# A two-block transformer kernel: the first input projection in another order, and four additions behind another weight piece

## The reference

```python
h = rmsnorm(x, norm_mix)
proj = h @ w_in                      # the first input projection
(m_z, m_xbc, m_dt, b_qkv, c_qkv, c_f, d_q, d_kv, gate_logits) = split(proj)
y_a = mamba2_branch(m_z, m_xbc, m_dt, ...)       # convolution of m_xbc, then a state space scan
y_b = moba_attention(b_q, b_k, b_v, ...)
y_c = forgetting_attention(c_q, c_k, c_v, c_f + forget_bias)
y_d = sliding_window_attention(d_q, d_k, d_v, ...)
x = x + sum(sigmoid(gate_logits) * (branches @ w_branch)) @ w_out
h = rmsnorm(x, norm_ffn)
x = x + (silu(h @ w_gate) * (h @ w_up)) @ w_down     # the first feed-forward
x = rmsnorm(x, norm_final)
```

## Time and profile before

| what | us |
|---|---|
| median of 3 runs (lowest, highest) | 928.53 (926.15, 930.83) |
| profiled execution | 926.62 |
| its span | 924.8 |
| PE busy | 907.0 |
| DVE busy | 685.7 |
| ACT busy | 509.9 |
| POOL busy | 103.9 |

### The profile page before, as it was taken

How to read it: one execution, slowest core, us unless ns; L and a number is a source line. 1 busy time by engine, 2 the same in 40 slices (tenths; PEclk the granted TensorE clock), 3 DMA queues, 4 the chain that set the end, 5 groups by cost and what they waited for, 6 DMA issues and landing times.

```text
span 924.8 us, 15609 instructions
## 1 busy us (share of the span) xinstructions
PE 907.0 (98%) x6262; PEld 771.2 (83%) x6262; DVE 685.7 (74%) x1116; ACT 509.9 (55%) x807; POOL 103.9 (11%) x114
## 2 busy tenths in 40 slices
PE   8999999999999999999999899999999999999998
PEld 8998887787778788888888689888988788888886
DVE  5876546566777768888788769678867578888886
ACT  5654446557854466555555574646436455565551
POOL 1000000131004100111000000003350003330000
PEclk9999999999999999999999999999999999999999
DMA  9769842244456535555544442231000445555631
GB/s 323 304 133 283 313 182 91 100 174 147 173 212 239 184 120 206 201 198 187 182 182 130 171 163 91 92 104 80 3 3 24 162 182 182 182 193 196 228 113 46
DMA packets 16871, 149.78 MB, mean 162 GB/s; under 512 B 1744, under 2 KB 6224, under 8 KB 8352
## 3 DMA queue, kind: packets, MB, share of 16 engines
q1 hardware_dynamic: 14688, 140.24, 41.0%
q0 software_dynamic: 1296, 5.24, 3.2%
q10 hardware_dynamic: 816, 3.31, 0.9%
HBM read 144.59 MB, written 4.19 MB: 161 GB/s over the span
## 4 chain that ended last, share of the span: by engine, by line
PE 87%; DVE 5%; ACT 3%; issue 2%; POOL 1%; DMA 1%; ACTq 0%; DVEq 0%; POOLq 0%
PE bank L774 41%; PE bank L816 17%; PE bank L818 9%; PE bank L731 4%; PE bank L1622 3%; PE bank L994 1%; POOL HN L3470 1%; DVE W_LOW L2484 1%; PE bank L1031 1%; PE bank L1068 1%; ACT W_HIGH L1856 1%; PE bank L899 1%; PE bank L1489 1%; DMA PRM<-params_dram 1%; PE bank L1383 0%
## 5 line engine op out<-in xcount | busy, mean ns | idle before, releaser
L2484 DVE TENSOR_TENSOR W_LOW<-weights,W_HIGH 128x2048 fp32r<-128x2048 f32 (+1 forms) x97 | 219.6, 2265 | 75.0 <-ACT W_HIGH L1856 74.1
L1856 ACT ACTIVATE W_HIGH<-weights 128x2048 fp32r<-128x2048 f32 (+1 forms) x97 | 181.5, 1872 | 105.8 <-PE bank L774 101.8
L816 PE MATMUL bank<-OVER_BOTH,W_HIGH 128*128 128x512 f32 x608 | 211.6, 392 | 0.2 <-DVE W_LOW L2484 0.2
L818 PE MATMUL bank<-OVER_BOTH,W_LOW 128*128 128x256 f32 x608 | 170.0, 280 | 0.0
L816 PEld LDWEIGHTS bank<-OVER_BOTH,W_HIGH 128*128 128x128 f32 x608 | 114.1, 188 | 25.9 <-DVE W_LOW L2484 0.5
L818 PEld LDWEIGHTS bank<-OVER_BOTH,W_LOW 128*128 128x128 f32 x608 | 114.2, 188 | 0.0
L1794 ACT ACTIVATE ARENA<-bank 128x256 f32<-128x256 f32 x88 | 33.6, 383 | 101.8 <-PE bank L818 101.0
L774 PE MATMUL bank<-GATE_HIGH,FIRST_BOTH 128*128 128x512 f32 x256 | 85.9, 400 | 1.0 <-DVE RING_LOW L2657 1.0
L774 PEld LDWEIGHTS bank<-GATE_HIGH,FIRST_BOTH 128*128 128x128 f32 x256 | 48.1, 188 | 11.6 <-DVE RING_LOW L2657 1.7
L774 PE MATMUL bank<-W_HIGH,HID_LOW 128*128 128x512 f32 x146 | 56.9, 390 | 0.0
L774 PE MATMUL bank<-W_LOW,HID_HIGH 128*128 128x512 f32 x146 | 56.9, 390 | 0.0
(11 more groups left out here) (580 smaller groups left out, 1932.5 us busy)
## 6 DMA issues: line engine op xcount, KB each, us to landing
weights<-weights_dram SPq DMA_DIRECT2D x62, 2048.0 KB, 8.1
weights<-weights_dram SPq DMA_DIRECT2D x3, 1024.0 KB, 9.0
bias_rows_dram<-ARENA POOLq DMA_DIRECT2D x1, 3072.0 KB, 39.5
BIAS<-params_dram ACTq DMA_DIRECT2D x1, 1997.0 KB, 14.6
weights<-weights_dram SPq DMA_DIRECT2D x1, 1664.0 KB, 6.6
weights<-weights_dram SPq DMA_DIRECT2D x1, 1584.0 KB, 6.8
weights<-weights_dram SPq DMA_DIRECT2D x3, 512.0 KB, 5.5
X<-x_dram ACTq DMA_DIRECT2D x2, 512.0 KB, 4.6
```

Of the source, the lines that this page charges most:

```text
L816: pe.matmul(o[:, :].rearrange("p (q n) -> p q n", q=2), high, both[:, :, k, :], start=(k == 0), stop=False, skip_group_check=True)
L818: ins = pe.matmul(o[:, 0:S], low, both[:, 0, k, :], start=False, stop=(k == KD - 1), skip_group_check=True)
L1856: act.activation(part_of(like_source(piece_parts(k)[0], k), k), part_of(piece_source(k), k), ACT.Copy)\
L2484: dve.tensor_tensor(low, part_of(src, k), high.bitcast(F32), ALU.subtract)\
```

## The change

The list of the first projection's chunks and jobs gets the order 0, 1, 2, 5, 9, 3, 4, 6, 7, 8, 10 (`IN1_ORDER`). Chunks 3 and 4 become wide like 6, 7 and 8. PE runs 5 and 9 by tokens where 3 and 4 stood, and then, behind `xs_T` and `cb`, the five wide chunks; the transposes of the rates come behind the first wide one, chunk 3. On ACT and DVE the takes, high and low parts follow that order. Apart from this, step 1 of `extras` of the first feed-forward stands one piece later. The pieces keep their count; by places in the new order 10 and 11 are chunk 3, 12 and 13 chunk 4.

```diff
--- before.py
+++ after.py
@@ -41,7 +41,8 @@
 LEVELS = 7
 
 
-CHUNKS = [("in1", i, w) for i, w in enumerate([KD * 384] + [KD * 512] * 10)]
+IN1_ORDER = (0, 1, 2, 5, 9, 3, 4, 6, 7, 8, 10)
+CHUNKS = [("in1", i, KD * (512 if i else 384)) for i in IN1_ORDER]
 CHUNKS += [("gate", i, KD * 512) for i in range(8)]
 CHUNKS += [("branch", i, 4 * D) for i in range(4)]
 CHUNKS += [("out1", i, KD * 512) for i in range(2)]
@@ -62,10 +63,10 @@
     return [(0, j, t) for t in range(2) for j in range(2)] + [(i, j, t) for i in range(1, chunks) for j in range(2) for t in range(2)]
 
 
-WIDE_IN = (6, 7, 8)
+WIDE_IN = (3, 4, 6, 7, 8)
 TILES = {"in1": [(i, j, t) for i in WIDE_IN for j in range(2) for t in range(2)], "ffn1": tiles_of(FF1_CHUNKS),
          "ffn2": tiles_of(FF2_CHUNKS)}
-JOBS = [("in1", i, j, *t) for i in range(11) for j in range(2) for t in (((0,), (1,)) if i in WIDE_IN else ((),))]
+JOBS = [("in1", i, j, *t) for i in IN1_ORDER for j in range(2) for t in (((0,), (1,)) if i in WIDE_IN else ((),))]
 JOBS += [("gate", i, j) for i in range(8) for j in range(2)]
 JOBS += [("branch", i, j) for i in range(4) for j in range(4)]
 JOBS += [("out1", i, j) for i in range(2) for j in range(2)]
@@ -934,9 +935,9 @@
             f_job_split("in1", 1, 0, *first)
             wait_fill_out(pe, ("table",))
             f_job_split("in1", 1, 1, *first)
-            for i in (2, 3):
-                f_jobs_split("in1", i, *first)
-            f_jobs_split("in1", 4, *first)
+            f_jobs_split("in1", 2, *first)
+            for i in (5, 9):
+                t_jobs_split("in1", i, *first)
             pe.wait_ge(sem("conv_done"), 8)
             for tt in range(TT):
                 o = open_fill(("xs_T", tt))
@@ -948,12 +949,12 @@
                 o = open_fill(("cb", g))
                 pe.matmul(o[:, 0:S], XBC[:, 4 + g, 0:P], XBC[:, 6 + g, :], start=True, stop=True)
                 close_fill(pe.matmul(o[:, S:384], XBC[:, 4 + g, P:S], XBC[:, 6 + g, P:S], start=True, stop=True))
-            for i in range(5, 11):
+            for i in (*WIDE_IN, 10):
                 if i in WIDE_IN:
                     wide_in(i)
                 else:
                     t_jobs_split("in1", i, *first)
-                if i == 5:
+                if i == WIDE_IN[0]:
 
                     pe.wait_ge(sem("rates_cumulated"), 1)
                     o = open_fill(("dt_T",))
@@ -1970,24 +1971,18 @@
             act.wait_ge(sem("params_halved"), 1)
             convs(0, 8)
             split_high(9)
-            take(("in1", 3, 0), flat(CQ1[:, 0:2, :]), 0.125)
+            take(("in1", 5, 0), CV1[:, 0, :])
             split_high(10)
             act.activation(EALOG[0:NH, :], prm("a_log")[0:NH, :], ACT.Exp).then_inc(sem("a_ready"), 1)
             softplus_parts(0, SPT)
-            take(("in1", 4, 0), flat(CK1[:, 0:2, :]))
+            take(("in1", 9, 0), BV1[:, 0, :])
+            split_high(11)
             for g in range(2):
                 take_fill(("cb", g), CB[:, g, :], 384)
-            split_high(11)
-            split_high(12)
-            take(("in1", 5, 0), CV1[:, 0, :])
-            split_high(13)
             for n, (i, j, t) in enumerate(TILES["in1"]):
-                cross_out("in1", n, (i, j, t), 1.0 if i == 8 else 0.125)
+                cross_out("in1", n, (i, j, t), 1.0 if i in (4, 8) else 0.125)
                 if t:
                     split_high(PIECE_AT["in1", i, j] + 2)
-            split_high(20)
-            take(("in1", 9, 0), BV1[:, 0, :])
-            split_high(21)
             gate_high(0)
             for tt in range(TT):
                 o = job_arrived(act, ("in1", 10, tt))
@@ -2610,7 +2605,7 @@
             convs(0, 8)
             minus_abs(SPX, SPT)
             split_low(9)
-            take(("in1", 3, 1), flat(CQ1[:, 2:4, :]), 0.125)
+            take(("in1", 5, 1), CV1[:, 1, :])
             split_low(10)
             softplus(0, SPX, SPT, SPX)
             dve.wait_ge(sem("consts_in"), 16)
@@ -2620,16 +2615,13 @@
             dve.tensor_tensor_scan(FCUM, ones[0:NH, :], SPX[:, S:2 * S], 0.0, ALU.mult, ALU.subtract)\
                 .then_inc(sem("rates_cumulated"), 1)
             split_low(11)
-            take(("in1", 4, 1), flat(CK1[:, 2:4, :]), 1.0)
+            take(("in1", 9, 1), BV1[:, 1, :])
             dve.wait_ge(sem("rates_cumulated"), 1)
             rows = SM8[0:NH, 768:1280]
             link(dve.tensor_scalar(DECAY_PARTS[:, :], ones[:, 0:1].to_broadcast([P, 512]), 0.0, None, ALU.mult))
             link(dve.tensor_copy(DECAY_PARTS[0:NH, :], rows))
             dve.tensor_tensor(DECAY_PARTS[32:32 + NH, :], rows, DECAY_PARTS[0:NH, :].bitcast(F32), ALU.subtract)\
                 .then_inc(sem("rows_ready"), 1)
-            split_low(12)
-            split_low(13)
-            take(("in1", 5, 1), CV1[:, 1, :], 1.0)
             o = fill_arrived(dve, ("dt_T",))
             dve.tensor_copy(DTT, o[:, 0:TT * NH])
             fill_out(dve.tensor_scalar(KEY_RATES, o[:, TT * NH:2 * TT * NH], -1.0, None, ALU.mult), ("dt_T",))
@@ -2642,12 +2634,10 @@
                 fill_out(dve.tensor_tensor(dst[1], src, bc(prm("d_skip", 0, NH).unsqueeze(2), [P, NH, HD]), ALU.mult),
                          ("xs_T", tt))
             for n, (i, j, t) in enumerate(TILES["in1"]):
-                add_cross("in1", n, (i, j, t), {6: DQ1, 7: BQ1, 8: BK1}[i][:, 2 * j + t, :], 1.0 if i == 8 else 0.125)
+                add_cross("in1", n, (i, j, t), {3: CQ1, 4: CK1, 6: DQ1, 7: BQ1, 8: BK1}[i][:, 2 * j + t, :],
+                          1.0 if i in (4, 8) else 0.125)
                 if t:
                     split_low(PIECE_AT["in1", i, j] + 2)
-            split_low(20)
-            split_low(21)
-            take(("in1", 9, 1), BV1[:, 1, :], 1.0)
             def gate_low(p):
 
                 if p >= len(GATE_PIECES):
@@ -2914,8 +2904,8 @@
             down1 = PIECE_AT["down1", 0, 0]
             for k in range(down1 + 2, in2 + 1):
                 split_low(k)
-                if k - down1 - last_of("down1") in (2, 3):
-                    extras("down1", EXTRA1, HALF_RSTD, CROSSED["ffn1"] + 4 * FF1_CHUNKS + 1, k - down1 - last_of("down1") - 2)
+                if k - down1 - last_of("down1") in (2, 4):
+                    extras("down1", EXTRA1, HALF_RSTD, CROSSED["ffn1"] + 4 * FF1_CHUNKS + 1, (k - down1 - last_of("down1")) // 4)
             dve.wait_ge(sem("late_in"), 32)
             for b in range(4):
                 tt, dc = divmod(b, 2)
```

## The result

The changed kernel takes 934.23 us (median of 5 runs, 933.24 to 935.62), the kernel before 928.1 us beside it (926.15 to 930.83). The ratio is 1.0067, with a 95% interval of 1.0054 to 1.008: slower by 0.7%, 6.1 us. The forecast was 935.1 us, slower. The profiled execution took 934.23 us, with a span of 932.4 us.

A forecast was written before the change was run, and what follows sets the result against it. TensorE (PE), busy 907.0 of 924.8 us, was taken as the bound. Projection +6.2, clock +1.7 and moved additions -1.3 us gave +6.6 us, 935.1 us on the median of 928.53, range 931.3 to 938.2 us.

The forecast's parts named there:

- PE's work and the way to the transposes: First projection up to the transposes of the rates: -0.4 and +0.4 us cancel, so PE comes through at 80.27 as before.
- The stop: Behind the transposes of the rates: PE waits 5.85 us on `W_LOW` while DVE works through its row.
- The clock: In PE's wait behind the transposes of the rates: clock falls, costing +1.7 us, bounds 0 to 3.4 us.
- The tail of the projection: From the transposes of the rates to the projection's end: four wide chunks and one token chunk cost +0.4 us.
- The additions behind the eleventh low part: First feed-forward: the wait moves from `DOWN_LOW` to `X`; gain between 0 and 2.8 us, taken as 1.3 us.
- The sum: Whole kernel: +6.2 + 1.7 - 1.3 = +6.6 us, 935.1 us on the median.
- the clock held in the stop: Rival at the transposes of the rates: clock stays up through PE's wait; +4.9 us, 933.4 us, chance 0.18.
- later waits gave nothing back: Rival claimed waits on `RING_LOW`, `MIX_LOW` and `DOWN_LOW` return time, with steady clock: +2.0 us, 930.5 us, chance 0.06.
- the rival with no stop: Rival at the transposes of the rates: chunk 4's low part is ready in time; -1.0 us, 927.6 us, chance 0.06.
- the rival with a late rise and nothing from the additions: Rival: clock behind the transposes' wait costs 3.4 us, moved additions gain 0; +9.6 us, 938.1 us, chance 0.08.

The follow-up runs named there:

- Early transposes: Changed kernel with PE's four transposes of the rates behind the first tile of chunk 3 instead of all of it: 926.1 us, ratio 0.9979.
- four products less in the row: Changed kernel with DVE's four products from the `xs_T` banks moved behind chunk 4's first low part: 931.33 us, ratio 1.0036.
- the second execution: Profiled execution of the unaltered changed kernel, measured again beside the kernel with 24 idle products: median 934.19 us, ratio 1.0065.
- the additions back: Changed kernel with the first feed-forward's four additions again in front of the eleventh low part: 935.28 us, ratio 1.0082.
- the filled stop: Changed kernel with 24 idle products of the identity on PE behind the transposes of the rates: 932.36 us, ratio 1.0045.
- the comparisons: Three comparisons of kernels with and without the four additions moved behind the eleventh low part: 0.9, 1.4 and 1.9 us.
- the additions alone: Kernel before with only the first feed-forward's four additions moved behind the eleventh low part: 927.02 us, ratio 0.9991.
- the 44 idle products: Changed kernel with 44 idle products of the identity on PE behind the transposes of the rates: 936.57 us, ratio 1.0092.

## Why the prediction was right

**PE's work and the way to the transposes:** right. Chunks 5 and 9 run from 43.31 to 66.20, 22.89 us for the 23.15 us of the earlier trace rows, with a delay of 0.4 us in each of the two places where waits of 0.3 and 0.5 us were forecast (two products take 0.84 us from 54.10, for 0.45 beside them, and one takes 0.67 us from 59.95, for 0.23). The gain was put at 0.4 us, the start-to-start times give 0.3; the transposes come at 79.78, 0.1 us before their place in the kernel before, as the forecast had them.

**The stop:** right in place, cause and size. Forecast 5.85 us, a wait of 5.6 to 6.0 on `W_LOW`; PE's wait is 5.72 us, and the step from the transposes to the next product grew from 0.35 us to 6.13, 5.8 us. The sum of DVE's rows in before (5.71 us) was the right thing to price, because nothing but that row lies between: 5.64 us in the trace of after. Early transposes make it vanish, and four products less in the row shorten it by what they take, 2.4 us.

**The clock:** the fall was right, the term that was off is its price. The prediction took 3.9 us at the lower level, by the start of the kernel, for 1.7 us. In the profiled execution the level lasted until 92.0, 6.1 us into PE's work, for 2.7 us; in the second execution 4.6 us into it (85.79 to 90.44), which by the same pace is 2.1 us; on the medians 1.8 us. The profile with the additions back, whose code in the projection is that of the change, has it from 84.6 to 91.5, 5.8 us of PE's work. The term was within its bounds (0 to 3.4). Its error was to take one length from one place: what the clock costs is the work that happens to lie in the low stretch, and this differs from execution to execution. It also priced one fall only, and put nothing for one behind the longer wait on `X` that it forecast.

The Trainium skill (TensorE: Matmul & The Clock Gate, section "Why this matters for your kernels") speaks against long gaps between bursts of products, because an idle PE goes back to half rate. These traces agree: the change's stop shows 0.50, and the filled stop 1.00. They also show falls behind shorter waits, and some with no idle time ahead (last section).

**The tail of the projection:** +0.4 us was forecast for four wide chunks and a token chunk. From 85.91 to 144.96 are 59.05 us, against 55.88 before; less 2.7 us for the clock, that is +0.5 us.

**The additions behind the eleventh low part:** right in mechanism. Forecast 1.3 us, the wait moving from `DOWN_LOW` to `X` with 2 to 3 us there; the profile has 2.5 us there, 1.5 us come back, and the comparisons say 0.9 to 1.9. That the 1.5 us are kept in the profile of the change is luck: in its second profile the clock fell behind `X` and took 1.3 us of them (5.83 us to the next projection's first product, for 4.55).

**The sum:** 5.6 us at the restart, 3.2 us to the end of the projection and -1.5 us up to `X` make the 7.3 us at 530.27, and the span is 7.6 us longer. Forecast were 6.6 us. On the medians it is 6.1 us. The two differ most likely because the profiled execution of before had a mean clock of 0.999, one of the quick ones, while the runs of before around the median, at 0.997 or 0.998, pay for a fall somewhere too (below). The forecast for the median was 0.9 us high: 0.5 us of it in the sum, 0.4 us because the median of before came out at 928.1 in place of 928.53. That it came so close is in part luck: the profile's loss is 1.0 us more than the sum, by the clock's price, and the median of before, 1.5 us above its profiled execution, more than covers that.

**The rivals:** the clock held in the stop in neither profile of the change; `RING_LOW` still has its 1.0 us, so later waits gave nothing back; and the rival with no stop is what the early transposes make of the kernel. It was put at 1.0 us under the kernel before, and 1.9 us (0.21%) were measured. Of the rival with a late rise and nothing from the additions, the change's two profiles each show a part: the longer low stretch the first, the additions' gain all but lost the second.

## What to carry to other kernels

When an order is rewritten, read each engine's row from its wait on: everything behind a wait is as late as that wait's release, whether it needs it or not. Here a low part with nothing to do with the rates stood behind DVE's wait for their transposes, and PE released that wait only when it had nothing left but that low part; four small instructions three tiles of chunk 3 earlier on PE turn a loss of 0.7% into a gain of 0.2%. Price a stop of TensorE at its own length plus a low clock for the work behind it, some 2 us here, and expect that second part to vary from run to run. A shorter wait that an edit moves to another place can bring such a fall too, as the one on `X` did here.

## What the hardware showed beyond this

The granted clock does not follow an idle time in a fixed way. It fell 1.6 us after PE had stopped in the profiled execution of the change, about 3.6 us after in a second one of the same kernel, and 4.7 us after in the one with the additions back, at the same stop of 5.7 us. A wait of 2.8 us left it at 1.00 in the kernel before; one of 2.46 us in the kernel with the additions alone, and one of 3.34 us in that with four products behind the low part, were followed by a fall, both only after PE was at work again. Its low stretch held 3.4 us of PE's work in these two, 4.6 and 6.1 us in the change. In the second block it fell at 666.7, 674.8 and 677.5 (early transposes, four products moved, the change's second profile) though PE's timeline shows no idle time in the ten microseconds ahead. What sets these times was not tried.

Much of the spread between runs goes with it. Of 23 runs of the kernel before, eleven at a mean clock of 0.999 or 1.0 took 926.0 to 927.0 us, nine at 0.997 or 0.998 took 927.9 to 928.8, and three at 0.994 or 0.995 took 929.6 to 930.8 us. On the other chip the two quicker groups touch: four runs at 0.999 took 926.5 to 927.7 us, twelve at 0.997 or 0.998 took 927.4 to 928.8. A gain of 1.5 us drowns in this unless the runs are many.

One thing stays open: where the transposes come early, and behind the 44 idle products, a pair of wide products takes 0.346 us and not 0.354. The profile with the additions back has 0.346 too, from where the clock rose again on, where the two profiles of the change with the same code have 0.354, so the order of the program alone does not set it. Over five wide chunks of 32 pairs that is 1.3 us, and no run tells why.
